# Order of the 512-column and 256-column products in the feed-forward's first matrix product: four and four in place of two and two

## The reference

```
def squared_relu_mlp(h, w1, w2):
    return jnp.square(jax.nn.relu(h @ w1)) @ w2
...
x = x + squared_relu_mlp(rms_norm(x, norm_ffn_g[l]), w_ff1[l], w_ff2[l])
```

## Time and profile before

| | |
|---|---|
| Median of three executions | 1600.52 us |
| The three | 1600.52, 1597.58, 1603.09 us |
| The profiled execution's own time | 1599.63 us |
| Span of its instructions | 1597.4 us |
| TensorE's mean granted clock in it | 0.998 |
| TensorE busy | 1585.6 us, 99% of the span |
| VectorE busy | 1318.6 us, 83% |
| ScalarE busy | 883.6 us, 55% |

### The profile page before, as it was taken

How to read it: one execution, slowest core, us unless ns; L and a number is a source line. 1 busy time by engine, 2 the same in 40 slices (tenths; PEclk the granted TensorE clock), 3 DMA queues, 4 the chain that set the end, 5 groups by cost and what they waited for, 6 DMA issues and landing times.

```text
span 1597.4 us, 22168 instructions
## 1 busy us (share of the span) xinstructions
PE 1585.6 (99%) x7914; PEld 1343.2 (84%) x7914; DVE 1318.6 (83%) x1759; ACT 883.6 (55%) x1116; POOL 93.1 (6%) x174
## 2 busy tenths in 40 slices
PE   9999999999999999999999999999999999999997
PEld 8888888888888888888888888888888888888886
DVE  5588989999998898786887787887879787978788
ACT  6444456555555566754566665455655455546545
POOL 6500010000000000000000000000000000000001
PEclk9999999999999999999999999999999999999999
DMA  7666655555555666657664576888678866987685
GB/s 255 202 188 187 191 153 182 170 174 173 182 176 182 200 201 186 198 178 250 211 191 152 176 231 178 281 254 291 186 254 253 277 218 217 288 263 236 183 287 194
DMA packets 169709, 337.47 MB, mean 211 GB/s; under 512 B 12425, under 2 KB 21249, under 8 KB 169217
## 3 DMA queue, kind: packets, MB, share of 16 engines
q1 hardware_dynamic: 164736, 325.62, 64.4%
q0 software_dynamic: 4864, 10.80, 3.2%
q10 hardware_dynamic: 32, 0.01, 0.0%
HBM read 326.95 MB, written 2.10 MB: 206 GB/s over the span
## 4 chain that ended last, share of the span: by engine, by line
PE 95%; DVE 3%; ACT 1%; issue 1%; DMA 0%; ACTq 0%; POOL 0%; POOLq 0%; DVEq 0%
PE ps L2476 15%; PE ps L1910 12%; PE ps L1912 12%; PE ps L1911 12%; PE ps L2185 8%; PE ps L2184 8%; PE ps L2183 8%; PE ps L2478 7%; PE ps L1923 1%; PE ps L2089 1%; PE ps L2303 1%; PE ps L2092 1%; DVE w_both L1165 1%; PE ps L2074 1%; PE ps L2073 1%; PE ps L2072 1%
## 5 line engine op out<-in xcount | busy, mean ns | idle before, releaser
L685 ACT ACTIVATE w_both<-raw 128x1024 fp32r<-128x1024 f32 x522 | 551.3, 1059 | 508.1 <-PE ps L1912 181.2
L1165 DVE TENSOR_TENSOR w_both<-raw,w_both 128x1024 fp32r<-128x1024 f32 x522 | 635.4, 1222 | 183.6 <-ACT w_both L685 181.9
L2476 PE MATMUL ps<-a_both,w_both 128*128 128x512 f32 x1024 | 321.8, 396 | 0.2 <-ACT rs_row L1087 0.2
L1910 PE MATMUL ps<-w_both,a_both 128*128 128x512 f32 x636 | 252.0, 396 | 0.1
L1912 PE MATMUL ps<-w_both,a_both 128*128 128x512 f32 x636 | 248.0, 390 | 0.0
L1911 PE MATMUL ps<-w_both,a_both 128*128 128x512 f32 x636 | 247.9, 390 | 0.0
L2478 PEld LDWEIGHTS ps<-a_both,w_both 128*128 128x128 f32 x1024 | 192.4, 188 | 45.4
L1226 DVE SCALAR_TENSOR_TENSOR acc<-hconv,cwk,acc 128x256 f32<-128x256 f32 x464 | 205.1, 497 | 7.4 <-PE ps L2128 7.4
L2478 PE MATMUL ps<-a_both,w_both 128*128 128x256 f32 x1024 | 201.2, 278 | 0.0
L2183 PE MATMUL ps<-w_both,c_hi 128*128 128x512 f32 x408 | 159.0, 390 | 0.0
L2185 PE MATMUL ps<-w_both,c_lo 128*128 128x512 f32 x408 | 158.8, 389 | 0.0
(11 more groups left out here) (412 smaller groups left out, 2214.1 us busy)
## 6 DMA issues: line engine op xcount, KB each, us to landing
raw<-in_w_ff_dram SPq DMA_DIRECT2D x224, 512.0 KB, 4.7
raw<-in_w_in_dram SPq DMA_DIRECT2D x144, 512.0 KB, 3.9
t_raw<-in_w_ff_dram SPq DMA_DIRECT2D x32, 1024.0 KB, 7.4
raw<-in_w_mla_out_dram SPq DMA_DIRECT2D x32, 512.0 KB, 4.1
raw<-in_w_conv_out_dram SPq DMA_DIRECT2D x32, 512.0 KB, 4.3
raw<-in_w_out_dram SPq DMA_DIRECT2D x32, 512.0 KB, 4.5
raw<-in_w_ukv_dram SPq DMA_DIRECT2D x16, 512.0 KB, 3.8
raw<-in_w_xkv_dram SPq DMA_DIRECT2D x16, 512.0 KB, 3.9
```

What stands on the lines that cost most here:

```text
L685: act.activation(whi[:, s, :], raw[:, s, :], ACT.Copy).then_inc(hi_ready, 1)
L1165: dve.tensor_tensor(wlo[:, s, :], raw[:, s, :], whi[:, s, :].bitcast(F32), ALU.subtract).then_inc(lo_ready, 1)
L1910: pe.matmul(sum_, x_hi[:, k0 + k, tok], w_hi, start=(first and k == 0), stop=False)
L2476: pe.matmul(both, whi[:, s, cols[n]], a_both[:, :, k0 + k, :], start=(first and k == 0), stop=False)
```

## The change

In each 128-row block all four wide products are issued first, b = 0 to 3, and then all four narrow ones, b = 0 to 3. Counts, operands, banks, waits and increments stay as they are.

```diff
--- before.py
+++ after.py
@@ -2469,13 +2469,12 @@
                 b0 = CPB * (c % 2)
                 pe.wait_ge(lo_ready, u + 1 + r)
                 for k in range(2):
-                    for b in range(0, CPB, 2):
-                        cols = [slice(NC * k + P * n, NC * k + P * (n + 1)) for n in (b, b + 1)]
-                        for n in range(2):
-                            both = ps[:, b0 + b + n, :].rearrange("p (h s) -> p h s", h=2)
-                            pe.matmul(both, whi[:, s, cols[n]], a_both[:, :, k0 + k, :], start=(first and k == 0), stop=False)
-                        for n in range(2):
-                            mm = pe.matmul(ps[:, b0 + b + n, 0:SEQ], wlo[:, s, cols[n]], a_hi[:, k0 + k, :], start=False, stop=(last and k == 1))
+                    cols = [slice(NC * k + P * b, NC * k + P * (b + 1)) for b in range(CPB)]
+                    for b in range(CPB):
+                        both = ps[:, b0 + b, :].rearrange("p (h s) -> p h s", h=2)
+                        pe.matmul(both, whi[:, s, cols[b]], a_both[:, :, k0 + k, :], start=(first and k == 0), stop=False)
+                    for b in range(CPB):
+                        mm = pe.matmul(ps[:, b0 + b, 0:SEQ], wlo[:, s, cols[b]], a_hi[:, k0 + k, :], start=False, stop=(last and k == 1))
                 mm.then_inc(used, 1)
 
             def ff_group(g, r, first=False, last=False):
```

## The result

The changed kernel takes 1602.72 us (median of 22 runs), the kernel before 1600.24 us (22 runs): a ratio of 1.0016, 95% interval 1.0010 to 1.0021, which is 2.5 us more. The profiled execution took 1602.85 us with a span of 1600.6. The forecast was 0.17% more; this is 0.16%, and by the interval anything from 0.10 to 0.21%.

The account below looks back on a forecast made before the run. TensorE's own pace was taken to bound the kernel. +2.6 us for the block pace and +0.1 us for leaving stages made +2.7 us, 1603.3 us as a median (0.17% more), range 1598.0 to 1608.0 us.

Parts of the forecast that it names:

- What bounds the kernel: Whole kernel: TensorE, busy 99% of the span at full clock, sets the end by its own pace.
- Waits and buffers: nothing: In the changed stages: later use of `wlo`, earlier bank writes and bank distance win nothing; the stage's waits cost 0.2 us.
- any new wait of TensorE: Sign on TensorE: its waits should be as before, and a new one would show the prediction wrong.
- The one term: Pace of a 128-row block in the four stages: 1403 ns against 1393, 256 x 10.2 ns = +2.6 us.
- Leaving a stage: First 512-column steps behind each of four stages: 30 ns more each time, +0.1 us.
- The account of the term: In each block: full weight loads stick out 6.7 ns beside narrow products, on three of four rather than one of two.
- The lower bound: Block pace if wide products recovered and narrow ones all ran at 113.3 ns: 1373 ns, -20 ns, -5.1 us.
- Catch-up ends sooner: Rival on wide products behind narrow ones: fewer changes halve their cost; 1393 ns, 1600.5 us, or 1595.4 us; chance 0.15.
- Every standing operand from the weight tile: Rival on a block's loads from `w_both`: narrow steps 120 ns, wide 235 ns, +6.9 us, 1607.4 us; chance 0.11.
- The order is neutral: Rival on a block's products: each costs by its own operands, so nothing changes, 1600.5 us; chance 0.10.

Follow-up runs that it names:

- one and one: Against the changed kernel, one wide and one narrow product in turn, eight times a unit: 1603.97 us, ratio 1.0028, second stage 90.44 us.
- Eight and eight: Against the changed kernel, all eight wide products of both 128-row blocks, then all eight narrow ones: 1601.09 us, ratio 1.0002, second stage 89.36 us.
- lag: Against the changed kernel, wide and narrow products in turn, but no two successive ones sharing a bank: second stage 90.23 us, 1410 ns a block.
- the key and value experiment: Against the kernel before, key and value block reordered from four wide, four narrow to two and two: three blocks take 4.18 us in place of 4.21.
- 240 columns: Against the changed kernel, each narrow product moves 240 columns in place of 256: second stage 87.88 us, 1373 ns a block.

## Why the prediction was right

**What bounds the kernel.** Right. The stage's length came through in the time: one and one made each of three stages 1.28 us longer than before and the whole 3.7 us by the medians (0.18 to 0.38% by the interval, 2.9 to 6.1 us; four stages would be 5.1). Eight and eight made a stage 0.20 us longer, and its 0.02% (-0.07 to 0.11%) fits that but can't be told from nothing.

**Waits and buffers: nothing.** Right for the stages: no new wait in one, the same clock, banks of no effect (lag). The prediction had named any new wait of TensorE as a sign of being wrong. There is one, of line 1950, and that of line 2183 grew; both lie outside of the stages and aren't shown to come of the change.

**The one term, +10.2 ns a block.** Right by size: 1403 ns measured, +9.7 ns a block by the stage. It was taken from a stretch with the same sequence of sizes and loads, and the key and value experiment shows that such a stretch is a fair measure in both directions. That the whole time agrees to 0.6 us (1603.3 forecast, 1602.72 measured) is in part luck: by the interval the difference of the two kernels is 1.6 to 3.4 us.

**Leaving a stage.** Forecast 2.31 us for the ten steps behind it, measured 2.32; the share in the total, 0.1 us, is below what can be told in it.

**The account of the term: wrong**, though the number was right, in the step "a full weight load doesn't quite fit beside a narrow product: 6.7 ns stick out", and with it "the narrow row pays its 6.7 ns on three products of four rather than on one of two, and the wide row doesn't win all of it back". Its own arithmetic didn't reach the term: one more narrow step at 6.7 ns is 6.7 ns a block, and the wide row was to win some of that back, while the term was 10.2. Measured, the narrow row grew by 13 ns and the wide one shrank by 3. And the load is no floor (240 columns at 112.5 ns). In the changed kernel the four narrow steps take 0.47 to 0.48 us, as forecast, but one and one, where by this account nothing sticks out, is the dearest order, and eight and eight, where the most does, is cheaper than four and four. The sum didn't use this account, only its wording did, so the forecast survived it. The lower bound (1373 ns) did use it, by letting every narrow step run at 113.3 ns; with full loads and 256 columns no order came below 1393. The range's lower end has a slip of its own: 2.9 us below 1600.5 is 1597.6, not 1598.0.

**The rivals.** Catch-up ends sooner: not in four and four. Its narrow part was right (473 ns, measured 474), but it had the wide row at 0.92 us and that takes 0.93. Eight and eight, with half the changes again, does win back 0.42 of the 0.62 us a stage. Every standing operand from the weight tile: no, 1403 is the key and value block's own figure, with half of its loads from elsewhere. The order is neutral: no; seven orders of the same products take 1393 to 1413 ns. The formula that the Trainium skill gives (TensorE: Matmul & The Clock Gate, section Back-to-back issue gap) makes a step depend on its own columns alone; the section says itself that in a stream of loads and products both set the spacing. Here a wide step takes 0.23 to 0.24 us depending on its neighbours. The prediction says that the trace disagrees with the page "on both figures"; its and the earlier trace rows measure products, and no row of it measures how long a load takes.

**A rival that it didn't name** is the traffic of the other engines beside TensorE. No experiment varies it alone. But in the second stage it is the same in both kernels (VectorE busy 67.9 of 88 us before and 68.6 of 90 after, ScalarE 49.3 and 49.4, the DMA engines 75 and 76%), and stages two to four agree to 0.01 us in every kernel.

**What stays open** is why. The runs show that the pace of a product depends on the sizes and loads of some products before it (at the end of the changed kernel's stage, for up to ten steps), that a stage's length repeats to 10 ns, and that it is no matter of the shared PSUM bank or of the particular operands. They don't show by what the earlier products act on the later ones. No single rule that I wrote down (a load as floor, a load paid each time, a cost per change of size, a slow pace handed on by full loads) gives the whole table; the order with the shortened loads contradicts each.

No order tried beats two and two, so the kernel before stays the best of these. Against the undisturbed paces of the earlier trace rows at most the table's excess could be won, and for two and two that is 33 ns of 1393.

## What to carry to other kernels

Where TensorE never waits, the order of its products is worth a look, but a small one: rearranging 2048 products of 7914 moved the time by 0.16%, and at the most, with one and one, by 0.28%. Price such a change by a stretch of the trace with the same sequence of moved and standing columns, read from start to start over many blocks, and not by adding up single steps from rows of equal products; the busy time of a line can fall while it gets slower. And test undoing a part: here, undoing the change in every second block brought nothing. A right number doesn't prove the reason given for it: here a stretch with the same sequence gave the number, and the experiments refuted the reason.

## What the runs showed of the hardware that was not expected

- One and one is the slowest order: 1413 ns for four products of 512 and four of 256 columns, where the undisturbed rows would make 1360. The expectation had been 1360 to 1370.
- Narrow steps at a full load of 128 columns take 112.5 ns for 240 moved columns and 120.0 for 256 (0.469 ns a column both), but 122.5 to 125 for 272 (0.45 to 0.46). With a load of 64 columns 256 take 113.3 ns (0.443 a column), and wide steps in a row take 0.443 with the full load (226.8 ns for 512).
- Behind eight narrow products five 512-column steps are slow, by 0.03 us together; behind four narrow ones ten steps take 0.05 us too long. The longer row leaves less behind.
- With the narrow loads halved, two and two went from 89.16 to 89.99 us a stage and four and four from 89.78 to 88.78. Less work made the first slower.
